# Ten V slots instead of eight, room taken from the output weights, and layer 2's modulation moved ahead of the first V gathers

## The reference

```
mod = silu(c) @ w_ada[l] + b_ada[l]          # 1024 x 6144: sh1, sc1, gt1, sh2, sc2, gt2
h = x * (1 + sc1) + sh1
mix = concat(mla, conv, swa)(h @ w_in[l]) @ w_o[l]
x = layer_norm(ALPHA * x + (1 + gt1) * mix)
h = x * (1 + sc2) + sh2
q = h @ w_pq[l]; top 16 of 128 x 128 product keys per head (8 heads) -> e, softmax gate g
a = gelu(sum(h * u_tab[e]))                  # one gathered row of 1024 per token, head and pick
y = sum(g * a * v_tab[e])
x = layer_norm(ALPHA * x + (1 + gt2) * y)
```

## Time and profile before

| | us |
|---|---|
| median of 3 runs | 1795.98 (1793.22 to 1796.22) |
| the profiled execution | 1794.02 |
| its span | 1792.2 |
| TensorE busy | 1223.0 (68%) |
| VectorE busy | 1082.5 (60%) |
| ScalarE busy | 412.0 (23%) |
| GpSimd busy | 984.4 (55%) |
| moved by DMA | 667.13 MB, 372 GB/s over the span |

### The profile page before, as it was taken

How to read it: one execution, slowest core, us unless ns; L and a number is a source line. 1 busy time by engine, 2 the same in 40 slices (tenths; PEclk the granted TensorE clock), 3 DMA queues, 4 the chain that set the end, 5 groups by cost and what they waited for, 6 DMA issues and landing times.

```text
span 1792.2 us, 16179 instructions
## 1 busy us (share of the span) xinstructions
PE 1223.0 (68%) x4938; PEld 546.0 (30%) x4938; DVE 1082.5 (60%) x3103; ACT 412.0 (23%) x995; POOL 984.4 (55%) x1044
## 2 busy tenths in 40 slices
PE   5986548789665668778766567788666555565555
PEld 2564423354222223255222123355222121121111
DVE  0046575666677667565677566565675776666642
ACT  1462111453210012344130012354120020110100
POOL 2000266656565556655665566556666666666663
PEclk8987759889878779888978788999968787788678
DMA  9978699999999999999999999999999999999996
GB/s 357 331 279 329 224 340 404 405 383 358 391 397 401 410 397 391 402 378 330 405 400 401 409 405 406 405 379 337 386 373 405 384 374 390 388 377 377 364 373 247
DMA packets 217191, 667.13 MB, mean 372 GB/s; under 512 B 21586, under 2 KB 50611, under 8 KB 217106
## 3 DMA queue, kind: packets, MB, share of 16 engines
q0 software_dynamic: 148240, 538.63, 77.7%
q1 hardware_dynamic: 68866, 127.46, 19.5%
HBM read 664.97 MB, written 1.05 MB: 372 GB/s over the span
## 4 chain that ended last, share of the span: by engine, by line
PE 24%; DVE 22%; DMA 18%; issue 12%; POOL 10%; another core or an unknown queue 9%; ACT 4%; SPq 1%; DVEq 0%; POOLq 0%; ACTq 0%
DMA ring<-in_u_tab,uidx 11%; DVE ring L1227 9%; PE y L1666 9%; DMA ring<-in_v_tab,vidx 6%; POOL ring L629 5%; POOL ring L617 4%; PE m L1377 4%; PE qb L1611 2%; PE m L1554 2%; ACT rows L786 1%; DVE ring L979 1%; DVE junk L1203 1%; DVE junk L1201 1%; PE m L1522 1%
## 5 line engine op out<-in xcount | busy, mean ns | idle before, releaser
L1666 PE MATMUL y<-ring,place 128*32 128x512 f32 x2048 | 617.5, 736 | 301.9 <-DMA ring<-in_v_tab,vidx 188.1
L617 POOL DMA_INDIRECT ring<-in_u_tab,uidx x512 | 490.9, 959 | 531.2 <-DVE ring L1227 203.1
L1227 DVE SCALAR_TENSOR_TENSOR ring<-ring,hp 128x1024 f32<-128x1024 f32 x512 | 613.8, 1214 | 265.8 <-DMA ring<-in_u_tab,uidx 170.8
L629 POOL DMA_INDIRECT ring<-in_v_tab,vidx x512 | 483.7, 945 | 257.1 <-issue 139.9
L1666 PEld LDWEIGHTS y<-ring,place 128*32 128x32 f32 x2048 | 122.1, 123 | 617.1 <-issue 612.7
L1611 PE MATMUL qb<-wpq,hT 128*128 128x256 f32 x512 | 140.6, 416 | 9.2 <-DVE vidx L1248 9.2
L1611 PEld LDWEIGHTS qb<-wpq,hT 128*128 128x128 f32 x512 | 99.0, 206 | 81.6 <-issue 69.9
L846 ACT ACTIVATE cdiag<-cst,wdT 128x128 f32<-128x128 f32 x248 | 80.3, 391 | 73.3 <-PE m L1554 52.1
L1377 PE MATMUL m<-win,hT 128*128 128x480 f32 x186 | 85.6, 602 | 2.5 <-ACT hT L699 2.4
L901 ACT ACTIVATE gexp<-best,nbest 128x16 f32<-128x16 f32 x32 | 9.8, 308 | 311.4 <-DVE nbest L1194 155.5
L1554 PE MATMUL m<-cdiag,hc 128*128 128x128 f32 x496 | 72.8, 287 | 5.4 <-issue 4.8
(11 more groups left out here) (234 smaller groups left out, 1269.2 us busy)
## 6 DMA issues: line engine op xcount, KB each, us to landing
ring<-in_w_ada SPq DMA_DIRECT2D x32, 1024.0 KB, 11.2
wpq<-in_w_pq SPq DMA_DIRECT2D x28, 1024.0 KB
win<-in_w_in SPq DMA_DIRECT2D x31, 720.0 KB, 20.8
wo<-in_w_ada SPq DMA_DIRECT2D x16, 1024.0 KB
wo<-in_w_o SPq DMA_DIRECT2D x32, 512.0 KB
ring<-in_u_tab,uidx POOLq DMA_INDIRECT x512
ring<-in_v_tab,vidx POOLq DMA_INDIRECT x512
xs<-in_x SPq DMA_DIRECT2D x1, 1024.0 KB, 14.0
```

The lines of the kernel that those rows point to most:

```text
L617: nc.gpsimd.indirect_dma_start(out=ring[:, n % UR, :], out_offset=None, in_=u_flat, in_offset=bass.IndirectOffsetOnAxis(ap=uidx[:, g % 2, ...
L629: nc.gpsimd.indirect_dma_start(out=ring[:, UR + n % VR, :], out_offset=None, in_=v_flat, in_offset=bass.IndirectOffsetOnAxis(ap=vidx[:, g ...
L1227: v.scalar_tensor_tensor(ring[:, n % UR, :], ring[:, n % UR, :], 1.0, HP[:, :], ALU.mult, ALU.mult, accum_out=dots[:, g % 2, k:k + 1]).the ...
L1666: e = mm(Y[n][lo:lo + QUAD, :], place[:, g % 2, run_of(k), :], ring[:, UR + (g * TOPK + k) % VR, n * 512:(n + 1) * 512], start=g % PH == 0 ...
```

## The change

`ring` gets ten V slots, and `wo` shrinks from four pieces to two. All twelve chunks of layer 2's modulation are now done before the first V gather: 0 to 6 by VectorE as before, in other places and at other slots, and 7 to 11 as products on TensorE into the PSUM bank `Y[0]`, with ScalarE's copy and TensorE's columns behind each. All columns are gathered in one PSUM bank, and one job of VectorE (`later_modulation`) adds the offsets for the whole layer. Chunks 9, 10 and 11 share one place: each load waits for the product of the chunk before it. Block 0 holds all its eight output weights at once (two in `wo`, six in slots of `ring` that no gather uses yet); blocks 1 to 3 reload through two places. Some of layer 1's chunks are loaded and multiplied earlier or later, and the first query weights are loaded after chunk 9 of layer 1. The first U gather waits for the products of chunks 7 and 8, the first V gather for all columns of layer 2, V gather 8 for layer 1's last chunk, and the first weighing for `later_modulation`.

```diff
-VR = 8
+VR = 10
...
-WO_SLOTS = 4
+WO_SLOTS = 2
...
-EARLY = 7
-ADA_SECOND = ((-91.8, 0.4, -85.75, -85.15), (-88.6, 0.35, -82.8, -81.8), (-85, 0.45, -79, -78), (-81, 0.9, -73, -72),
-              (-73.8, 0.9, -65.9, -65.1), (-64.5, 0.6, -59, -58), (-58, 1, -48, -47), (84, 0.7, 92, 95), (96, 0.7, 104, 107),
-              (108, 0.7, 116, 119), (214, 0.7, 222, 225), (226, 0.7, 234, 237))
+SUMS = 6
+ADDED = 7
+SUM_START = ((45.1, 0.18), (46.6, 0.18), (48.1, 0.55), (54.95, 0.4), (58.5, 1.0), (67, 1.6), (76, 0.3))
+SUM_USED = ((45.3, 46.2), (47, 47.6), (50.5, 52.5), (57.2, 60.5), (64, 68), (72, 75.3))
+COLUMN_SLOT = (53.36, 53.37, 57.6, 75.2, 75.3, 104.1, 104.2)
+SECOND_SLOT = {7: -35.5, 8: -35, 9: -26, 10: -15, 11: -8}
...
-    return ADA_SECOND[c][0] + ADA_SECOND[c][1] * n
+    return tuple(BASE[0] + at for at in ((23.2, 23.9, 24.4, 24.9), (23.6, 25.5, 26.1, 26.6), (35.4, 35.8, 38.2, 38.7),
+                                         (45.1, 45.4, 45.9, 46.4), (46.5, 47.2, 47.6, 47.95),
+                                         (53.32, 53.8, 54.25, 54.9))[c - 4])
...
-        wo_w = [view(wo, j * D, D) for j in range(WO_SLOTS)]
+        wo_w = [view(wo, j * D, D) for j in range(WO_SLOTS)] + [ring[:, j, :] for j in (14, 15, 8, 9, 10, 11)]
...
-            [view(wo, b * half_n, KC // 2, ADA_N) for b in range(2)]
+            [view(wo, 0, KC // 2, ADA_N), view(ring_all, 7 * half_n, KC // 2, ADA_N)]
...
+        def ada_pair(c):
+
+            return c % 2 if c < ADDED else 1 if c == ADDED + 1 else 2
 
         def ada_place(l, c, half):
 
-            if l and c >= EARLY:
-                return 6 + half, 4 + c - EARLY
-            if l == 0 and (c == 3 or c >= 10):
-                return 6 + half, max(1, c - 8)
-            n = 9 + c if l else c - (c > 3)
-            return n % 3 * 2 + half, n // 3 + 1
+            if l:
+                pair = ada_pair(c)
+                return pair * 2 + half, (2, 2, 4)[pair] + sum(ada_pair(i) == pair for i in range(c + 1))
+            if c in (3, 7) or c >= 10:
+                return 6 + half, (3, 7, 10, 11).index(c) + 1
+            return ((0, 1, 2, None, 0, 1, 2, None, 2, 2)[c] * 2 + half, (1, 1, 1, None, 2, 2, 2, None, 3, 4)[c])
...
+        def wo_slot(m, j):
+
+            return j if m == 0 else j % WO_SLOTS
 
...
-            return ring_all[:, 6 * half_n + c % 2 * ADA_N:6 * half_n + (c % 2 + 1) * ADA_N] if c < EARLY else rowbuf[:, :]
+            b = c % SUMS
+            if b < 4:
+                return ring_all[:, 6 * half_n + b * ADA_N:6 * half_n + (b + 1) * ADA_N]
+            return place[:, b - 4, :, :].rearrange("p a b -> p (a b)")
 
...
         Q_BANK = bank("qb")
...
+        def summed(eng, ops, chain, c, n):
+
+            to, by = sums_of(c), ccol[:, n:n + 1]
...
+                eng.wait_ge(s[f"ada_in{place_}"], 16 * held)
+            if n == 0 and c >= SUMS:
...
+            w = ada_places[place_][:, n % 4, :]
+            if n == 0:
+                chain(ops.tensor_scalar(to, w, by, None, ALU.mult))
+                return
...
+            e = ops.scalar_tensor_tensor(to, w, by, to, ALU.mult, ALU.add)
...
+            def first_output_weights():
+                yield BASE[0] + 45.6
+                full(sp, ("ad", 7))
+                for j in range(4):
+                    wo_load(0, j)
+                yield BASE[0] + 53.5
+                full(sp, ("ad", 9))
+                for j in range(4, KC):
+                    wo_load(0, j)
...
+                full(sp, after)
...
                     yield BASE[m] + 60 + 2 * (j - WO_SLOTS)
-                    sp.wait_ge(s["wo_used"], WO_SLOTS * m + j - WO_SLOTS + 1)
+                    sp.wait_ge(s["wo_used"], (KC - WO_SLOTS) * (m - 1) + j - WO_SLOTS + 1)
                     wo_load(m, j)
 
...
-                yield BASE[0] + 25
+                for k in range(2):
+                    yield ada_slot(k + 4)[0] + 0.5
+                    full(sp, ("ad", k + 4))
+                    ada_load(1, k)
+                for k in range(8, 10):
+                    yield ada_slot((6, 8)[k - 8])[0] + 0.5
+                    full(sp, ("ad", (6, 8)[k - 8]))
+                    ada_load(0, k)
                 for hd in range(2):
                     wpq_load(0, hd)
...
+            def second_modulation():
+                for c in range(2, ADDED):
+                    for half in range(2):
+                        yield BASE[0] + SUM_USED[c - 2][half]
+                        added(sp, c - 2, half)
+                        ada_load(1, c, half)
+                yield BASE[0] + 74.5
+                full(sp, ("w1", 0))
+                ada_load(1, 7)
+                yield BASE[0] + 76.9
+                added(sp, 5, 1)
+                ada_load(1, 8)
+                for c, before in ((9, 7), (10, 9), (11, 10)):
+                    yield SECOND_SLOT[before] + 0.1
+                    sp.wait_ge(s["mod_full"], before - ADDED + 1)
+                    ada_load(1, c)
...
-                full(sp, ("w1", 1))
-                ada_load(1, EARLY)
...
 
-            upto = in_slot_order(startup(), output_weights(0, BASE[0] + 20, lambda e: full(e, ("ad", 3))), first_keys(),
+            upto = in_slot_order(startup(), first_output_weights(), second_modulation(), first_keys(),
                                  input_weights(1, -62, ("sk3", 0)), query_weights(),
-                                 output_weights(1, 30, lambda e: full(e, ("ad", 11))), second_layer(),
+                                 output_weights(1, 30, ("ad", 11)), second_layer(),
                                  input_weights(2, BASE[2] - 20, ("pw", 1)),
-                                 output_weights(2, BASE[2] + 33, lambda e: added(e, 9, 1)),
+                                 output_weights(2, BASE[2] + 30, ("w1", 1)),
                                  input_weights(3, BASE[3] - 20, ("sk3", 2)),
-                                 output_weights(3, BASE[3] + 30, lambda e: added(e, ADA_CHUNKS - 1, 1)), stores())
+                                 output_weights(3, BASE[3] + 30, ("w1", 2)), stores())
             upto(LAST_SLOT + LAG)
...
+                elif n == 8:
+                    full(pool, ("ad", 11))
...
-            full(pool, ("ad", 9))
-            added(pool, EARLY - 1, 1)
+            added(pool, ADDED - 1, 1)
+            pool.wait_ge(s["mod_full"], 2)
             for n in range(-TOPK, TURNS * TOPK + LAG):
                 if n + TOPK < TURNS * TOPK:
                     gather_u(*divmod(n + TOPK, TOPK))
                 if n == LAG:
-                    full(pool, ("as", 1, EARLY - 1))
+                    pool.wait_ge(s["mod_sums"], ADA_CHUNKS)
...
+                    if k == 10:
+                        act.wait_ge(s["mod_sums"], 11)
+                    elif k == 11:
+                        act.wait_ge(s["mod_sums"], ADA_CHUNKS)
...
+            def second_rows():
+                for c in range(ADDED, ADA_CHUNKS):
+                    yield SECOND_SLOT[c] + 0.2
...
+                        act.wait_ge(s["mod_sums"], c)
...
+            def later_modulation():
+                yield -3
+                dve.wait_ge(s["mod_sums"], ADA_CHUNKS)
+                chain(v.tensor_tensor(modc[:, 1, :], MOD_SUMS, colT[:, COLS_B:2 * COLS_B], ALU.add))
+                chain.sync()
+                fold(1, SC1, SH1, ln_cols(G_LN2, 0), ln_cols(B_LN2, 0))
+                fold(1, SC2, SH2, ln_cols(G_LN1, 1), ln_cols(B_LN1, 1))
+                chain.sync()
+                dve.sem_inc(s["cols_ready1"], 1)
...
+            def products_of(l, c, bank):
+
+                for k in range(KC):
+                    if k % 4 == 0:
+                        place_, held = ada_place(l, c, k // 4)
+                        pe.wait_ge(s[f"ada_in{place_}"], 16 * held)
+                    w = ada_places[place_][:, k % 4, :]
+                    q = k % 4 * QUAD
+                    e = mm(bank[q:q + QUAD, :], ccol[:, k:k + 1].to_broadcast([P, QUAD]), w,
+                           start=k < P // QUAD, stop=k >= KC - P // QUAD, tile_position=(0, q))
+                return e
...
+                for c in range(ADA_CHUNKS):
+                    if c < ADDED:
+                        yield BASE[0] + COLUMN_SLOT[c]
+                        added(pe, c, 1)
+                    else:
+                        yield SECOND_SLOT[c]
+                        if c > ADDED:
+                            pe.wait_ge(s["mod_rows"], c - ADDED)
+                        products_of(1, c, Y[0]).then_inc(s["mod_full"], 1)
+                        yield SECOND_SLOT[c] + 0.3
+                        pe.wait_ge(s["mod_rows"], c - ADDED + 1)
+                    if c == 0:
+                        pe.wait_ge(s["cols_out"], 1)
+                    src, by = (sums_of(c), ones[:, 0:1]) if c < ADDED else (rowbuf, pick_rows)
                     for q in range(ADA_C):
-                        e = mm(bank[:, q:q + 1], sums_of(k)[:, q * P:(q + 1) * P], ones[:, 0:1], start=True, stop=True)
```

(61 more changed lines are left out.)

124 lines of the change are left out of this document (38 added, 86 removed).

## The result

On the chip of the first comparison the changed kernel took 1829.63 us in the median of 4 runs (1819.32 to 1837.25), the kernel before 1794.6 us (1790.49 to 1796.22, 4 runs): a ratio of 1.0199 [1.0152, 1.0247], 35 us slower. I had said 1765. The profiled execution took 1827.76 us. The ratios of this document leave out two executions that lie far above the others of their kernel, 3413.29 us of v10_d8 and 2002.08 us of a_stall_again; nothing on record says what held the first.

The account below looks back on a forecast made before the run. The prediction saw a startup with holes, then gathers at or near the DMA ceiling from the first V gather on. Its sum was 1794.0 - 26 + 0 - 13 + 10 = 1765 us, range 1738 to 1790.

Parts of the forecast that it names:

- part 3: Ten V slots for the gathers: fewer GpSimd pauses in the late stretch, minus 13 us, bounds 0 to 26.
- Part 1: Layer 2's modulation chunks 7 to 11 leave the stretches where DMA is full: minus 26 us.
- part 2: Same chunk loads moved into the startup, and its new order: 0 at the first V gather, two sides cancelling.
- Turns 4 to 6: Sign of being right: these turns some 16 us shorter, as three of the five moved chunks had loaded there.
- The 12.4 us: Startup waits of TensorE for chunk sums and a reloaded output weight, expected off the path to the first U gather.
- Late next is chunk 11: Startup: the last chained modulation chunk was named as the next thing to come late.
- Part 4: Two places for output weights in blocks 1 to 3: nine reload waits of 6 us, a fifth showing, plus 10 us.
- the 10 us of room: Output products of blocks 1 to 3: two product steps leave about 10 us for a reload.
- The U slots bind: Rival: GpSimd waits more for the six U slots, so the added V slots give 0; 1778 us, chance 0.16.
- Slower, by the reloads: Rival: output-weight reloads in blocks 1 to 3 outlast their room by 11 us, nine times; 1818 us, chance 0.08.

Follow-up runs that it names:

- v10_d8: Changed kernel with its ten V places but at most eight V gathers out at once: 1782.37 us, 0.9849 of the kernel before.
- a_stall_again: Changed kernel with 40 repeated copies of the query rows on ScalarE in each second turn, second measurement: 1983.09 us, 1.0967 of the kernel before.
- u8_v8_third: Changed kernel with eight U and eight V slots instead of six and ten: 1758.02 us, 0.9728 of the kernel before, which took 1810.35 us.
- b_w2: Kernel before with only two places for the output weights in blocks 1 to 3: 1740.02 us, 1.0009 of the kernel before.
- v8_w2_third: Changed kernel with eight V slots instead of ten, two output-weight places kept: 1778.27 us, 0.9864 of the kernel before, which took 1802.56 us.
- after_again: Changed kernel itself, measured again on another chip: 1708.25 us against 1739.07 us of the kernel before, 0.9829.
- after_third: Changed kernel itself, measured a third time: 1836.46 us against 1805.39 us of the kernel before, 1.0192.

## Why the prediction was wrong

**The step that failed is part 3**: "Bounds 0 to 26, I take half: minus 13". It measures plus 59 on an 1800 chip, and minus 4.5 on a 1739 chip (1708.25 against 1712.73). Two things in it were wrong. I let the worst case be a gain of nothing on the ground that added slots "only lengthen" a queue, and that is no reason: the V gathers share GpSimd with the U gathers, and a V gather sent two rows earlier changes which of the two it stops at. I had written that part of each pause would move to the U side; it came back there twice over. The very rows I quoted had the warning, 203.1 us ahead of U gathers against 116 us ahead of V gathers. And I read one pause (2.99 us ahead of a V gather) as the pattern; that rate of 379 GB/s was the mark of an 1800 chip, not of missing V slots. The fastest kernel there, u8_v8_third, has 382 GB/s from 1290 to 1680 us.

**Part 1, minus 26: right.** The modulation's move alone is 1738.33 - 1710.1 = 28 us on the one kind and 0.0139 x 1803 = 25 us on the other, both with part 2 in it. Turns 4 to 6 were to be 16 us shorter: V gather 64 to V gather 112 takes 140.6 us on the 1739 chip,

```profile
414.80 0.94 POOL L668 DMA_INDIRECT ring<-in_v_tab,vidx  x1 [0.30 <-issue]
...
555.39 0.93 POOL L668 DMA_INDIRECT ring<-in_v_tab,vidx  x1 [0.30 <-issue]
```

against 156.6 us in b_w2 (418.3 to 574.9). In the first comparison it shows as only 1.7 us (150.8 before, 149.1 after); with eight slots on an 1800 chip it is 8.1 us (142.7, v8_w2_third). That the slots' loss hides the rest is a reading, not shown.

**Part 2, nothing at the first V gather: right to 0.3 us** (238.04 against 238.28), part of it luck, for on the 1739 chips the first V gather is 4 us earlier than in b_w2 (234.58 against 238.58). The 12.4 us came through at the first U gather (189.44 against 201.49), and the wait for chunk 11 took them back, as said ("Late next is chunk 11"): VectorE stopped for the last columns, and the next U gather came 11.73 us late.

```profile
233.91 0.21 DVE L1051 TENSOR_TENSOR modc<-y,colT 128x48 f32<-128x48 f32 x1 [10.06 <-PE y L1395]
...
236.79 0.94 POOL L654 DMA_INDIRECT ring<-in_u_tab,uidx  x1 [11.73 <-DVE ring L1266]
```

**Part 4, plus 10: too large.** On a 1739 chip the two places cost 1.7 us in the kernel before (b_w2) and 3.6 us beside the new modulation (1713.67 - 1710.1); on an 1800 chip they cost 0.0003 of the time, nothing. TensorE waited 8.7 us in all for output weights in the first comparison,

```profile
PE m L1575 <- DMA wo<-in_w_o: 8.7, 4, 3.2
```

2.8 us on a 1739 chip, and 14.2 to 18.8 us in the later traces with two places and no added pauses on 1800 chips, where I had nine waits of 6 us. The chain of waits has three of the reloads, from issue to landing:

```profile
861.77 6.51 DMA wo<-in_w_o
887.84 6.48 DMA wo<-in_w_o
...
1308.77 6.64 DMA wo<-in_w_o
```

The DMA is full during all three (407 to 408 GB/s), and the page of after_again has the same for all 26 of its loads:

```profile
wo<-in_w_o SPq DMA_DIRECT2D x26, 512.0 KB, 7.0
```

I had taken 16 us, from input weights issued five in a row, where the landing of one holds the time of those ahead of it. The rule of the Trainium skill that I set against the rows (DMA: Bandwidth & Descriptors, "Queues, rings and completion order") has each engine serve its queues in turns and makes this part 0. The landings fit it better than my 16 us does: 6.5 us lie inside the 10 us of room, though they are more than the 2.6 us that half of the rate would give. No run shows the turns themselves.

**The rivals.** "The U slots bind" named the right slots. I priced it at 0 for part 3, where its mechanism gives a loss as soon as the V side is let further ahead. "Slower, by the reloads" had the right sign and the wrong mechanism: its pauses at the output products are not what the slots' kernels differ in. My case for slower needed TensorE to stand still; what the runs showed is the wait of one issuer for two sets of slots.

**What stays open.** Why the U side loses more than the V side wins is argued, not shown: the gathers leave in a fixed order, so where V slots are scarce GpSimd stops with U rows in hand, and VectorE has products to do while TensorE catches up; where they are plenty it stops only when VectorE, too, has come to wait in its order for TensorE (for the mask add, the picks, the places), and then no U row is on its way when it goes on. The five sums above fit this; no run took VectorE's waits away by themselves. Why the same slots cost 59 us on one kind of chip and gain 4.5 us on the other is open too, beyond the full DMA of the second.

## What to carry to other kernels

Where one issuer alternates between two streams with a set of slots each, choose the two depths together: here two slots lost 59 us on one side and gained 24 us on the other (0.9864 against 0.9728). Try the side the issuer waits for longest first, and price both signs for the other. Before a change to buffering is judged, run the kernel before and the changed one on several chips; a rate that one chip shows (379 GB/s here) may be that chip's. The version to keep of those tried is eight U and eight V slots with the new modulation, 0.9844 on the one kind of chip, level with ten V slots there (0.9829, the intervals overlap), and 0.9728 on the other, faster than the kernel before on both.

## What the runs showed of the hardware

**Two kinds of chip.** Bytes and instructions of the changed kernel are the same in both. The slower kind isn't slower in its instructions (in after_third against after_again a VectorE product takes 1213 ns against 1216, a gather 949 ns of GpSimd against 954) but in what lies between them. TensorE's mean granted clock is lower, 0.808 against 0.853, and a matmul of the output products (L1575) takes 683 ns against 616, but all of TensorE's busy time is only 6 us more (1228.2 against 1222.1). One such place in after_third, around the copy of the query rows:

```profile
1289.63 1.03 PE L1664 MATMUL qb<-wpq,hT 128*128 128x256 f32 x4
...
1292.43 1.98 PE L1575 MATMUL m<-wo,hT 128*128 128x512 f32 x4
...
1301.96 0.93 POOL L654 DMA_INDIRECT ring<-in_u_tab,uidx  x1 [0.30 <-issue]
1306.13 0.81 SPq L520 DMA_DIRECT2D wo<-in_w_o  x2
1306.19 0.37 ACT L938 COPY qrow<-qb 128x256 f32<-128x256 f32 x1 [23.98 <-remote]
1306.51 0.94 POOL L668 DMA_INDIRECT ring<-in_v_tab,vidx  x1 [3.61 <-remote]
...
1306.62 0.69 PE L1673 MATMUL qb<-cst,qrow 128*128 128x128 f32 x2 [12.21 <-ACT qrow L938]
```

ScalarE waits by the code for the query product, whose last four matmuls the trace has from 1289.63; SyncE for the output product at 1292.43; GpSimd for a weighing. All three go on within 0.4 us of each other, 12 to 16 us after those matmuls end in the trace, as if TensorE's signals had been held back together. On a 1739 chip the same copy follows with nothing between:

```profile
1210.70 1.03 PE L1664 MATMUL qb<-wpq,hT 128*128 128x256 f32 x4
...
1211.77 0.37 ACT L938 COPY qrow<-qb 128x256 f32<-128x256 f32 x1 [12.37 <-PE qb L1664]
```

What holds them is not in the records, and no run tries it. The 1800 chips' traces also lack about half of the signals that the others' have (10,883 in after_third against 23,461 in after_again), so a "remote" there may be only a lost record, and some TensorE times may be early. As every execution here was taken down by the profiler, no run excludes that the recording itself takes part in the pauses.

**The sign of a change can hang on the chip**: 0.9829 [0.981, 0.9849] on one, and 1.0192 [1.0157, 1.0227] and 1.0199 [1.0152, 1.0247] on two others for the same program, each interval far from 1.
